# Down phases of an encoder step: block sums made in place, operands prepared earlier, ends re-ordered, and matmuls of a tile ordered by column halves

## The chip, the cores and the metric

The kernel runs on 1 core of one Trainium2 chip. The metric is device time in microseconds (us). TensorE (PE in the rows; PEld are its weight loads), VectorE (DVE), ScalarE (ACT), GpSimd (POOL) and SyncE (SP, which only issues transfers here) each run a program of their own in order and meet at semaphores.

## The reference

Two layers of an encoder over 1024 prompt rows and 32 sample rows (1056 columns here), width 1024. Each layer is a mixer and then a feed-forward part, in fp32:

```
def sq_relu_ffn(h, w1, w2):
    return jnp.square(jax.nn.relu(h @ w1)) @ w2
xp = xp + mp
xp = xp + sq_relu_ffn(rms_norm(xp, norm_ffn_g[i]), w_ffn1[i], w_ffn2[i])   # w1 1024x4096, w2 4096x1024
```

The change lies in the second product (the "down phase") of both layers, and in what follows it: in layer 0 the norm and input projection of the next mixer, in layer 1 the transposes and the output.

## The kernel before, in words

Every fp32 product is made of three float32r matmuls: both operands are split into a high part (ACT copies to float32r) and a low part (the difference), and high·high, high·low and low·high are summed.

**Up phase.** 16 units of 256 hidden rows, two jobs (128 rows) each. SP loads a unit's weights into one half of `stage`, POOL splits them (`split`: four high pieces of 512 columns, then four low ones) into one half of `w_sp`, PE runs 72 matmuls of 352 columns a job (L273), DVE takes the relu and scales it (L433), ACT squares (`squares`, L358). Hidden rows and columns are cut into halves, and DVE forms sums of the blocks (`combine`, L441 to L446) so that the down product takes 7 block products instead of 8 (Strassen–Winograd). SP stores a unit's 8 blocks in memory (`hid_spill`, 2112 KB).

**Down phase.** 8 chunks of K; a chunk has 7 block products q, each of 4 tiles m, so 28 tiles. A tile (`down_tile`, L317) is 12 matmuls of 264 columns into a pair of PSUM banks; the four pairs are used in turn. For each chunk:

- SP loads two stage halves of weights (`down_weights`, L1996) once POOL has made the low part for q = 6 of the chunk before, and then the hidden blocks (`hidden`, L2000), each once PE is done with that q.
- POOL (`split_down`) makes the sums of weight blocks that a q needs (two 512-column sums, L2136 to L2142) and the low parts of the weights (L2149). ACT makes the high parts (`w_high`, L371) and those of the hidden blocks (`b_high`, L376); DVE makes the low parts of the hidden blocks (`b_low`, L460).
- DVE adds each finished tile to its target (`down`, L468 and L470), x in `xT` or one of three sums in `aux`. PE may be at most four tiles ahead of it (`pt_free`).

The engines' programs are written out by hand, so the order is that of the code. ACT's `prepare` handles `w_high(c, q)`, then `b_high(c, q - 1)`. DVE has one or two `b_low` behind the four `down` of a q: in chunk 0 behind q = 4 it has `b_low(7)` and `b_low(8)`, which belong to q = 0 and 1 of chunk 1, and behind q = 5 `b_low(9)` and `b_low(10)`.

Sums for q = 2, 3 and 6 go to two buffers `Sx`, which lie over `rstd`, the scale that DVE still reads for the last up unit; so POOL waits there for both of its jobs. The operands for q = 2 and 3 lie over the `w_sp` half of the last or the last but one up unit; those for q = 6 lie over the buffer from which the last up unit is stored.

**The last chunk** runs its tiles by m: all 7 q for m = 0, then m = 1 and so on (`LAST`). When DVE has the seven, it and POOL (`combine_last`, L2164 to L2170) add up the block sums of that m. DVE's seventh `down` waits for all four of POOL's additions. In layer 0 POOL runs `split(U_OIN)`, which prepares the weights of the next projection, ahead of all `combine_last`. SP loads these weights behind the last `down_weights`. ACT and DVE put the next norm's squares and the split of x between (`act_n2`, `dve_n2`).

Of the kernel before, what the change touches and what calls it, by code (L numbers as in the profile page):

```python
# [74 lines left out]
BLK = [0, 2, 4, 5, 6, 7, 3]  # L75
S_AT = {2: 0, 3: 1, 4: 2, 6: 3}
# [3 lines left out]
SC_S = sum(P * (b + 1) for b in range(2, 8))  # L80

# [6 lines left out]
def build_encoder(nc, dram):  # L88
    ctx = ExitStack()
    with ctx:  # L90
# [123 lines left out]
        cb, cb_u, cb_x = sem("cb"), sem("cb_u"), sem("cb_x")  # L214
# [66 lines left out]
        def gemm_in_unit(pe, u, j, widths=(P, P), du=0, dj2=0, blk=None, rhs=lambda k, b: h[:, k, b, :]):  # L281

            pe.wait_ge(w_split, u + 1 + du)
            for t, m in enumerate(widths):
                gemm_tile(pe, j + t, u % 2, KT, t * P, 256, m, rhs, dj2,
                          blk if t == 0 else None)

        def pe_up(pe, u0, j0, blkh, times):
            pe.wait_ge(w_split, u0 + 1)
            gemm_tile(pe, j0, u0 % 2, KT, 0, 256, P, ffn_h, blk=blkh)  # L290
# [7 lines left out]
            gemm_tile(pe, j0 + 1, u0 % 2, KT, P, 256, P, ffn_h)  # L298
# [11 lines left out]
        def down_tile(pe, L, t, q, m, dt=0):  # L310
# [35 lines left out]
        LAST = [0, 1, 2, 3, 4, 5, 6]  # L346

        def act_ffn(act, L, j0):
# [5 lines left out]
            def squares(i, d=0):  # L354
                for t in range(2):
                    evacuated(act, j0 + 2 * i + t, d)
                    x = ob[i % 2][:, 2 * t:2 * t + 2, :]
                    act.activation(x, x, ACT.Square).then_inc(s_done, 1)  # L358

            def w_high(c, q, d=0):  # L360

                K = NCHK * L + c
                slot = (L + 0) % 2
                for i in range(2):
                    st = stage[:, (slot + i) % 2, :]
# [4 lines left out]
                    x = {0: st[:, 0:512], 1: st[:, 1024:1536], 4: st[:, 512:1024], 5: st[:, 1536:2048]}.get(q, Sx[i][:, :])  # L370
                    act.activation(w2[q][i][:, 0, :], x, ACT.Copy).then_inc(wh_done, 1)  # L371
# [16 lines left out]
            squares(0)  # L388
            with act.Fori(0, 7) as i:
                for t in (1, 2):  # L390
                    squares(t + 0, i * 2)
            for q in (0, 1):
                w_high(0, q)
            for q in (0, 1):
# [269 lines left out]
        def dve_n2(dve, ch):  # L664
# [1666 lines left out]
```

## Time and profile before

| what | value |
|---|---|
| median of 3 runs | 2571.79 us (2571.58 to 2573.43) |
| the profiled execution: its own time | 2571.93 us |
| its span in the trace | 2570.2 us |
| mean granted clock of TensorE | 0.983 of full speed |
| PE busy | 2456.9 us (96%), 17227 matmuls |
| POOL busy | 1413.0 us (55%) |
| DVE busy | 1456.5 us (57%) |
| ACT busy | 777.5 us (30%) |

Layer 0's down phase begins at about 928 us of the span and layer 1's at about 2199 us. PE's busy time of 96% hides stretches in which it stands still; they are in the rows below. A clock of 1.00 in a row is 2.4 GHz, 0.50 is 1.2 GHz.

### The profile page before, as it was taken

How to read it: one execution, taken by the hardware profiler on the slowest of the kernel's cores; microseconds unless marked ns; L12 is line 12 of the kernel's file. 1: busy time of each engine (PE TensorE's matmuls, PEld its weight loads, DVE VectorE, ACT ScalarE, POOL GpSimd, SP SyncE). 2: the span in 40 equal slices, each digit the busy share in tenths (PEclk: the TensorE clock that was granted, in tenths of full speed). 3: DMA queues.
4: the chain of work that ended last, by engine and by line, in shares of the span. 5: the costliest groups of instructions: out<-in, count | busy, mean ns of one | idle time of the engine just before them, and what ended most of it. 6: DMA issues, size and time to landing. Idle time of an engine off the chain costs nothing.

```text
span 2570.2 us, 42362 instructions
## 1 busy us (share of the span) xinstructions
PE 2456.9 (96%) x17227; PEld 2322.9 (90%) x17227; DVE 1456.5 (57%) x1988; ACT 777.5 (30%) x1164; POOL 1413.0 (55%) x1035
## 2 busy tenths in 40 slices
PE   8999999999999997999889999989999999799998
PEld 7998866999999997999878998669999999799998
DVE  4333389444333465776668878763433343667676
ACT  4200277211010123333237832652110101243431
POOL 4433256245444558787751333953554454688785
PEclk9999999999999998999999998999999999999999
DMA  6111110213344444445140111002134433444441
GB/s 221 34 50 35 69 66 2 84 50 134 123 143 150 149 154 142 158 125 158 55 141 23 50 34 55 18 17 101 46 138 150 150 127 140 193 125 143 158 126 77
DMA packets 128201, 264.10 MB, mean 103 GB/s; under 512 B 15517, under 2 KB 81141, under 8 KB 123478
## 3 DMA queue, kind: packets, MB, share of 16 engines
q1 hardware_dynamic: 125446, 245.17, 28.2%
q10 hardware_dynamic: 2640, 17.31, 1.7%
q8 instruction: 83, 1.36, 0.2%
q14 instruction: 32, 0.26, 0.0%
HBM read 173.72 MB, written 87.93 MB: 102 GB/s over the span
## 4 chain that ended last, share of the span: by engine, by line
PE 62%; POOL 17%; issue 11%; DVE 7%; ACT 2%; DMA 0%; POOLq 0%; SPq 0%; DVEq 0%; ACTq 0%
PE PS L273 49%; POOL w L2149 9%; POOL Sx L2142 2%; POOL Sx L2138 1%; PE PS L1097 1%; PE PS L1158 1%; POOL Sx L2136 1%; PE PS L1508 1%; PE PS L317 1%; PE PS L1135 1%; POOL stage L2140 1%; PE PS L1537 1%; PE PS L1477 1%; POOL Lb L1872 1%; PE PS L780 1%
## 5 line engine op out<-in xcount | busy, mean ns | idle before, releaser
L273 PE MATMUL PS<-h,w_sp 128*128 128x352 f32 (+1 forms) x5184 | 857.1, 325 | 16.2 <-DVE h L726 6.6
L273 PEld LDWEIGHTS PS<-h,w_sp 128*128 128x128 f32 (+1 forms) x5184 | 839.3, 188 | 23.3 <-issue 18.0
L2104 POOL TENSOR_TENSOR w_sp<-stage,ones 128x512 fp32r<-128x512 f32 x244 | 268.2, 1131 | 835.8 <-PE PS L273 788.8
L317 PE MATMUL PS<-Bq,w 128*128 128x264 f32 x5376 | 667.3, 287 | 51.1 <-DVE xT L470 42.5
L317 PEld LDWEIGHTS PS<-Bq,w 128*128 128x128 f32 x5376 | 664.2, 191 | 54.1 <-issue 26.6
L273 PE MATMUL PS<-hz,w_sp 128*128 128x352 f32 x3456 | 567.0, 323 | 0.0
L273 PEld LDWEIGHTS PS<-hz,w_sp 128*128 128x128 f32 x3456 | 557.7, 188 | 0.0
L2108 POOL TENSOR_TENSOR w_sp<-stage,w_sp 128x512 fp32r<-128x512 f32 x244 | 368.6, 1542 | 0.0
L433 DVE SCALAR_TENSOR_TENSOR ob<-PS,rstd 128x1056 f32<-128x1056 f32 x64 | 80.5, 1258 | 400.1 <-PE PS L273 400.1
L358 ACT ACTIVATE ob<-ob 128x1056 f32<-128x1056 f32 x64 | 69.6, 1088 | 643.7 <-DVE ob L433 643.7
L2149 POOL TENSOR_TENSOR w<-stage,w 128x512 fp32r<-128x512 f32 x128 | 191.6, 1520 | 131.4 <-ACT w L371 131.2
L470 DVE TENSOR_TENSOR xT<-PS,xT 128x528 f32<-128x528 f32 x256 | 177.9, 704 | 109.8 <-PE PS L317 85.4
L460 DVE TENSOR_TENSOR Bq<-Bq 128x1056 fp32r<-128x1056 f32 x112 | 177.1, 1585 | 37.0 <-ACT Bq L376 37.0
L470 DVE TENSOR_TENSOR aux<-PS,aux 128x528 f32<-128x528 f32 x168 | 117.9, 704 | 65.7 <-PE PS L317 65.6
L2149 POOL TENSOR_TENSOR w<-Sx,w 128x512 fp32r<-128x512 f32 x96 | 139.3, 1471 | 0.0
L376 ACT ACTIVATE Bq<-Bq 128x1056 fp32r<-128x1056 f32 x112 | 119.3, 1074 | 40.1 <-PE PS L317 36.7
L371 ACT ACTIVATE w<-Sx 128x512 fp32r<-128x512 f32 x96 | 60.8, 633 | 215.2 <-POOL Sx L2136 72.3
L1234 POOL TENSOR_TENSOR sg<-sg,kept 128x1024 f32<-128x1024 f32 (+3 forms) x45 | 82.2, 1829 | 63.3 <-DVE kept L1204 63.0
L973 DVE TENSOR_TENSOR Z<-PS,rstd 128x1056 f32<-128x1056 f32 x20 | 25.1, 1257 | 159.7 <-PE PS L273 155.3
L371 ACT ACTIVATE w<-stage 128x512 fp32r<-128x512 f32 x128 | 75.1, 626 | 129.4 <-DMA stage<-in_w_ffn 69.7
L1571 ACT ACTIVATE reach<-score,bs__92 128x1024 bf16<-128x1024 f32 (+2 forms) x96 | 99.0, 1033 | 12.8 <-DVE bs__92 L1717 12.2
L1704 DVE TENSOR_SCALAR_CACHE_REDUCE reach<-score,bs__92 128x640 bf16<-128x640 f32 (+3 forms) x128 | 88.6, 745 | 1.6 <-DVE bs__92 L1694 0.2
(307 smaller groups left out, 2310.6 us busy)
## 6 DMA issues: line engine op xcount, KB each, us to landing
hid_spill<-ob SPq DMA_DIRECT2D x32, 2112.0 KB, 7.6
stage<-in_w_ffn SPq DMA_DIRECT2D x64, 1024.0 KB, 7.5
Bq<-hid_spill SPq DMA_DIRECT2D x112, 528.0 KB, 3.8
stage<-in_w_in_even SPq DMA_DIRECT2D x10, 1024.0 KB, 4.8
stage<-in_w_in_odd SPq DMA_DIRECT2D x9, 1024.0 KB, 5.0
x_spill<-xT ACTq DMA_DIRECT2D x2, 4224.0 KB, 12.6
xT<-x_spill ACTq DMA_DIRECT2D x2, 4224.0 KB, 12.5
xtok<-in_x_prompt SPq DMA_DIRECT2D x8, 512.0 KB, 8.9
```

Of the source, the lines that this page charges most:

```text
L273: mm = pe.matmul(out[0:m, c, :], lhs, rhs(k, b)[:, c * CH:(c + 1) * CH], start=(i == 0 and n == 0), stop=(i == nk - 1 and n == 2))
L317: mm = pe.matmul(out[:, c, :], w2[q][i][:, a, m * P:(m + 1) * P], Bq[q][:, b, i, c * QN:(c + 1) * QN], start=(i == 0 and n == 0), stop=(i ...
L371: act.activation(w2[q][i][:, 0, :], x, ACT.Copy).then_inc(wh_done, 1)
L376: act.activation(Bq[q][:, 0, :, :], B_raw[q][:, :, :], ACT.Copy).then_inc(bh_done, 1)
L460: dve.tensor_tensor(Bq[q][:, 1, :, :], B_raw[q][:, :, :], Bq[q][:, 0, :, :].bitcast(F32), ALU.subtract).then_inc(bl_done, 1)
L470: ins = dve.tensor_tensor(x, src, x, ALU.add)
L1234: pool.tensor_tensor(w, w, x[:, :, c0 + 1:c0 + 1 + n], ALU.mult).then_inc(a_w, 1)
L1571: act.activation(reach[:, r], score[:, r], ACT.Sign, scale=-1.0, bias=bs_[:, n % 2, bi:bi + 1], accum_out=bs_[:, 2, bi:bi + 1]).then_inc(a ...
L1704: ch.mark(dve.tensor_scalar(reach[0:m, r], score[0:m, r], bs_[0:m, now, bi:bi + 1], 0.0, ALU.is_lt, ALU.add, accum_out=bs_[0:m, CNT, bi:bi ...
L2104: pool.tensor_tensor(w_sp[:, s, 0, q:q + 512], stage[:, s, q:q + 512], ones[:, 0:1].to_broadcast([P, 512]), ALU.mult).then_inc(w_hi_done, 1)
L2108: lo = pool.tensor_tensor(w_sp[:, s, 1, q:q + 512], stage[:, s, q:q + 512], w_sp[:, s, 0, q:q + 512].bitcast(F32), ALU.subtract)
L2149: pool.tensor_tensor(w2[q][i][:, 1, :], x, w2[q][i][:, 0, :].bitcast(F32), ALU.subtract).then_inc(wl_done, 1)
```

## The change

In words:

- **Block order.** The products are renumbered (`BLK`, `S_AT`, new `A_AT`): q = 0, 1, 2 now take a weight block as it lies in `stage`, q = 3 to 6 take sums, and these are made in place in `stage`; `Sx` is gone.
- **Stage half and `w_sp` half** of a unit come from `wslot`, which swaps the halves from U_OIN on. The operands for q = 2 and 3 now lie over the `w_sp` half of the last unit but one in both layers, so that ACT waits for two jobs less (`job_done, j0 + 30`).
- **Last up unit.** ACT squares its two halves between `w_high` steps, and POOL, not DVE, makes its four sums (`last_combine`), between its steps for q = 5 and q = 6.
- **Column order.** In `down_tile` the loop over the two column halves (banks) moves from innermost to outermost.
- **Last chunk.** `LAST` puts q = 2 next to last. DVE's last `down` of an m waits for three of POOL's additions and no longer for the fourth. In layer 0 POOL runs `combine_last(0)`, the high half of `split(U_OIN)`, `combine_last(1)`, the low half, and the other two. SP loads U_OIN one step later. The norm's additions and x splits on DVE are placed differently, and PE waits for one `pt_free` less.

The diff, cut:

```diff
-BLK = [0, 2, 4, 5, 6, 7, 3]
-S_AT = {2: 0, 3: 1, 4: 2, 6: 3}
+BLK = [0, 2, 7, 4, 5, 6, 3]
+S_AT = {3: 0, 4: 1, 5: 2, 6: 3}
+A_AT = [0, 2, 3, 3, 3, 1, 3]
+def wslot(u):
+    return (u + (u >= U_OIN)) % 2
...
-            for i in range(2):
-                for n, (a, b) in enumerate(((0, 0), (0, 1), (1, 0))):
-                    for c in range(2):
+            for c in range(2):
+                for i in range(2):
+                    for n, (a, b) in enumerate(((0, 0), (0, 1), (1, 0))):
                         mm = pe.matmul(out[:, c, :], w2[q][i][:, a, m * P:(m + 1) * P],
...
-        LAST = [0, 1, 2, 3, 4, 5, 6]
+        LAST = [0, 1, 3, 4, 5, 2, 6]
...
-            squares(15)
-            act.wait_ge(job_done, j0 + 32)
+            act.wait_ge(job_done, j0 + 30)
             w_high(0, 2)
             w_high(0, 3)
-            for q in range(2, 6):
-                b_high(0, q)
-            b_high(0, 6)
+            square(15, 0)
             act.wait_ge(hid_st[0], 16 * (8 * L + 8))
             w_high(0, 4)
             w_high(0, 5)
+            square(15, 1)
+            for q in range(2, 7):
+                b_high(0, q)
             act.wait_ge(hid_st[1], 16 * (8 * L + 8))
             w_high(0, 6)
...
-                    if q == 0 and m == 1:
-                        combine(15)
-                for n in ((2,), (3, 4), (5, 6), (), (7, 8), (9, 10), (11,))[q]:
+                for n in ((2,), (3,), (4,), (5, 6), (7, 8), (9, 10), (11,))[q]:
                     b_low(n)
...
-                dve.wait_ge(cb, 16 * L + 4 * m + 4)
+                dve.wait_ge(cb, 16 * L + 4 * m + 3)
                 down(t0 + 6, 6, m)
...
-                                evacuated(pool, (J_F0, J_F1)[L] + 30)
-                                evacuated(pool, (J_F0, J_F1)[L] + 31)
...
+            def last_combine(L):
+
+                x, n = ob[1], 4 * (16 * L + 15)
+                pool.wait_ge(s_done, 2 * (16 * L + 15) + 2)
+                pool.tensor_tensor(x[:, 4, :], x[:, 1, :], x[:, 0, :], ALU.subtract).then_inc(t_done, 1)
+                pool.tensor_tensor(x[:, 6, :], x[:, 3, :], x[:, 1, :], ALU.subtract).then_inc(t_done, 1)
...
+            def down_all(L):
+                split_down(0, L, qs=range(6))
+                last_combine(L)
+                split_down(0, L, qs=(6,))
...
-            down_all(0, U_F0)
-            split(U_OIN)
-            combine_last(0)
+            down_all(0)
+            pool.wait_ge(job_done, J_F0 + 32)
+            combine_last(0, 0)
+            split_high(U_OIN)
+            combine_last(0, 1)
+            split_low(U_OIN)
+            combine_last(0, 2)
+            combine_last(0, 3)
```

How the programs stand, first POOL at the beginning of layer 0's down phase, before (`w_2_0` is the operand for q = 2, K half 0; `Sx` the sum buffers):

```order
L2149 TENSOR_TENSOR w_1_1_66<-stage,w_1_1_66 128x512
L2136 TENSOR_TENSOR Sx_77<-stage 128x512
L2136 TENSOR_TENSOR Sx_78<-stage 128x512
L2149 TENSOR_TENSOR w_2_0_67<-Sx_77,w_2_0_67 128x512
L2149 TENSOR_TENSOR w_2_1_68<-Sx_78,w_2_1_68 128x512
L2138 TENSOR_TENSOR Sx_77<-Sx_77,stage 128x512
L2138 TENSOR_TENSOR Sx_78<-Sx_78,stage 128x512
```

and the same stretch, up to q = 6, in the changed kernel:

```order
L2151 TENSOR_TENSOR w_2_0_67<-stage,w_2_0_67 128x512
L2151 TENSOR_TENSOR w_2_1_68<-stage,w_2_1_68 128x512
L2141 TENSOR_TENSOR stage<-stage 128x512 x2
...
L2151 TENSOR_TENSOR w_5_0_73<-stage,w_5_0_73 128x512
L2151 TENSOR_TENSOR w_5_1_74<-stage,w_5_1_74 128x512
L2158 TENSOR_TENSOR ob_52<-ob_52 128x528
L2159 TENSOR_TENSOR ob_52<-ob_52 128x528
L2161 TENSOR_TENSOR ob_52<-ob_52 128x528
L2163 TENSOR_TENSOR ob_52<-ob_52 128x528
L2147 TENSOR_TENSOR stage<-stage 128x512 x2
L2151 TENSOR_TENSOR w_6_0_75<-stage,w_6_0_75 128x512
```

The low parts for q = 2 now follow at once, and the four sums of the last up unit (`ob_52`) stand ahead of q = 6.

POOL at the end of layer 0's down phase, before (`w_sp` is the split of the next projection's weights):

```order
L2104 TENSOR_TENSOR w_sp<-stage,ones 128x512 x4
L2108 TENSOR_TENSOR w_sp<-stage,w_sp 128x512 x4
L2164 TENSOR_TENSOR xT<-xT,aux 128x528
L2165 TENSOR_TENSOR xT<-xT,aux 128x528
L2168 TENSOR_TENSOR xT<-xT,aux 128x528
L2170 TENSOR_TENSOR xT<-xT,aux 128x528
```

and in the changed kernel:

```order
L2179 TENSOR_TENSOR xT<-xT,aux 128x528
L2180 TENSOR_TENSOR xT<-xT,aux 128x528
L2183 TENSOR_TENSOR xT<-xT,aux 128x528
L2185 TENSOR_TENSOR xT<-xT,aux 128x528
L2109 TENSOR_TENSOR w_sp<-stage,ones 128x512 x4
L2179 TENSOR_TENSOR xT<-xT,aux 128x528
```

The additions for m = 0 have moved ahead of the split, whose halves now stand behind m = 0 and m = 1.

## Rows read from the trace of the kernel before

**Rows 1.** PE by stretch: length, busy us (matmuls), granted clock, DMA share, GB/s

```profile
927.80:990.50 62.70, 43.62 (x338) 0.91 0.47 172
1000.00:1040.00 40.00, 40.00 (x332) 1.00 0.47 145
1237.80:1310.30 72.50, 56.09 (x409) 0.91 0.16 56
2199.30:2260.70 61.40, 43.46 (x338) 0.90 0.47 176
2507.80:2553.90 46.10, 41.55 (x337) 0.98 0.04 12
```

**Rows 2.** Timeline, start of layer 0's down phase: start, us, what, count [idle before]

```profile
907.80 6.46 POOL L2149 TENSOR_TENSOR w<-stage,w 128x512 fp32r<-128x512 f32 x4 [15.18 <-ACT w L371]
...
929.37 2.56 POOL L2136 TENSOR_TENSOR Sx<-stage 128x512 f32<-128x512 f32 x2 [15.10 <-issue]
...
937.66 0.36 SPq L1985 DMA_DIRECT2D hid_spill<-ob  x1
...
956.40 2.55 POOL L2149 TENSOR_TENSOR w<-Sx,w 128x512 fp32r<-128x512 f32 x2
...
957.73 1.62 SPq L1996 DMA_DIRECT2D stage<-in_w_ffn  x2
...
966.39 1.67 ACT L371 ACTIVATE w<-stage 128x512 fp32r<-128x512 f32 x3 [3.33 <-DMA stage<-in_w_ffn]
...
969.07 1.65 DVE L460 TENSOR_TENSOR Bq<-Bq 128x1056 fp32r<-128x1056 f32 x1 [6.18 <-ACT Bq L376]
...
978.61 7.68 PE L317 MATMUL PS<-Bq,w 128*128 128x264 f32 x48 [10.66 <-DVE xT L470]
...
990.47 19.71 PE L317 MATMUL PS<-Bq,w 128*128 128x264 f32 x140 [4.18 <-DVE xT L470]
```

**Rows 3.** DMA issues of 935 to 970 us: count, KB, us to landing

```profile
hid_spill<-ob SPq DMA_DIRECT2D x1, 2112.0 KB, 6.4
```

**Rows 4.** The page's groups: count, busy us, mean ns of one, idle before

```profile
L470 DVE TENSOR_TENSOR xT<-PS,xT 128x528 f32<-128x528 f32 x256 | 177.9, 704 | 109.8 <-PE PS L317 85.4
L460 DVE TENSOR_TENSOR Bq<-Bq 128x1056 fp32r<-128x1056 f32 x112 | 177.1, 1585 | 37.0 <-ACT Bq L376 37.0
...
L376 ACT ACTIVATE Bq<-Bq 128x1056 fp32r<-128x1056 f32 x112 | 119.3, 1074 | 40.1 <-PE PS L317 36.7
```

**Rows 5.** POOL's low parts by source line: ns min/median/max

```profile
L2149 POOL TENSOR_TENSOR w<-stage,w x128: 1265/1299/2315, 907.8 to 2505.0; 128x512 fp32r<-128x512 f32 x128
```

**Rows 6.** Timeline, end of layer 0's down phase

```profile
1245.69 5.55 POOL L2104 TENSOR_TENSOR w_sp<-stage,ones 128x512 fp32r<-128x512 f32 x4 [2.38 <-DMA stage<-in_w_in_odd]
...
1256.11 1.29 POOL L2164 TENSOR_TENSOR xT<-xT,aux 128x528 f32<-128x528 f32 x1
...
1261.38 0.71 DVE L470 TENSOR_TENSOR xT<-PS,xT 128x528 f32<-128x528 f32 x1 [11.30 <-POOL xT L2170]
...
1262.14 23.64 PE L317 MATMUL PS<-Bq,w 128*128 128x264 f32 x180 [9.83 <-DVE xT L470]
...
1298.01 11.76 PE L273 MATMUL PS<-h,w_sp 128*68 128x352 f32 x72 [2.75 <-issue]
...
1310.26 1.98 PE L705 MATMUL PS<-rstd,ones 128*128 128x512 f32 x4 [0.49 <-DVE rstd L675]
```

**Rows 7.** Timeline, end of layer 1's down phase

```profile
2552.51 0.71 DVE L470 TENSOR_TENSOR xT<-PS,xT 128x528 f32<-128x528 f32 x1 [1.70 <-POOL xT L2170]
...
2553.88 10.63 PE L2293 MATMUL PS<-ident,xT 128*128 128x128 f32 x72 [3.63 <-DVE xT L470]
```

**Rows 8.** Timeline of PE and PEld: eight matmuls of one bank (L1372), 18 rotating (L273)

```profile
924.89 3.04 PE L273 MATMUL PS<-h,w_sp 128*128 128x352 f32 x18
...
1343.87 1.26 PEld L1372 LDWEIGHTS PS<-h,w_sp 128*128 128x128 f32 x8 [0.76 <-issue]
...
1343.87 1.55 PE L1372 MATMUL PS<-h,w_sp 128*128 128x352 f32 x8
```

More of the change, by code:

```diff
@@ L352, in act_ffn, with square @@
                                scale=1.0 / D).then_inc(rt_done, 1)
[L354 to L358, printed above, removed]
+            def square(i, t, d=0):
+                evacuated(act, j0 + 2 * i + t, d)
+                x = ob[i % 2][:, 2 * t:2 * t + 2, :]
+                act.activation(x, x, ACT.Square).then_inc(s_done, 1)
             def w_high(c, q, d=0):
                 K = NCHK * L + c
-                slot = (L + 0) % 2
                 for i in range(2):
-                    st = stage[:, (slot + i) % 2, :]
                     if q in S_AT:
@@ L386, in prepare @@
                         b_high(c, q - 1, d)
-            squares(0)
+            for i in range(1):
+                square(0, 0)
+                square(0, 1)
             with act.Fori(0, 7) as i:
[L390 to L394, printed above, removed]
-                b_high(0, q)
-            squares(15)
-            act.wait_ge(job_done, j0 + 32)
+                for n in (1, 2):
+                    square(n, 0, i * 2)
+                    square(n, 1, i * 2)
+            w_high(0, 0)
+            w_high(0, 1)
+            b_high(0, 0)
+            b_high(0, 1)
+            act.wait_ge(job_done, j0 + 30)
             w_high(0, 2)
             w_high(0, 3)
-            for q in range(2, 6):
-                b_high(0, q)
-            b_high(0, 6)
+            square(15, 0)
             act.wait_ge(hid_st[0], 16 * (8 * L + 8))
@@ L496, in dve_ffn, with last @@
                     b_low(7 + q + 5, i)
-            def last(m, before=()):
+            def last(m, one=None, two=None):
                 t0 = 196 + 7 * m
                 own = PT_L * L + t0
+                step = 4 * L + m + 1
                 a1, a5, a6 = (aux[:, m, x, :] for x in range(3))
@@ L505, in last @@
                 down(t0 + 1, 1, m)
-                down(t0 + 2, 2, m)
-                down(t0 + 3, 3, m)
+                down(t0 + 2, 3, m)
+                if one is not None:
+                    one()
+                down(t0 + 3, 4, m)
                 if m == 0:
@@ L523, in dve_ffn @@
             for m in range(4):
-                last(m)
-                if between is not None:
-                    between(m)
+                if between is None:
+                    last(m)
+                else:
+                    last(m, *between[m])
+            if between is not None:
+                between[4]()
         def x_tile_ready(eng, n, m):
@@ L1423, in pe_odd @@
             pe.wait_ge(w_split, U_OIN + 2)
[L1424 removed]
+            gemm_tile(pe, J_OI + 2, wslot(U_OIN + 1), KT, 0, 256, P, hh, between=kip_turns)
             evacuated(pe, J_OI + 1)
@@ L2192, in _ @@
             split_ffn(1, U_F1, 5)
-            down_all(1, U_F1)
-            combine_last(1)
+            down_all(1)
+            for m in range(4):
+                combine_last(1, m)
         @block.scalar
```

166 lines of the change are left out of this document (79 added, 87 removed).

## The prediction

> **What bounds the kernel now.** I read the windows of PE first, since they show where PE loses time. In the middle of a down phase it loses none: 332 matmuls in 40.00 us at full clock are 0.1205 us each, and busy is the whole window [rows 1]. A tile of 12 costs 1.45 us and a chunk of 28 tiles 40.5 us. Against that stand four stretches at the ends of the phases [rows 1]:
>
> - start of layer 0's phase up to the moment when chunk 1 begins: 62.7 us for one chunk, 22.2 too long;
> - the same in layer 1: 61.4 us, 20.9 too long;
> - layer 0's last chunk up to the norm's sum matmul: 72.5 us. It holds 40.5 us of tiles and the first job of the next projection, 11.8 us [rows 6], so 20.2 are lost;
> - layer 1's last chunk up to the transposes: 46.1 us, 5.6 lost.
>
> Together 68.9 us, which is also the most that the change can give there, apart from the clock and the output tail.
>
> The timeline then says who is late. In chunk 0 PE stands for 10.66 and 4.18 us for a DVE addition [rows 2]. That is PSUM room and no late operand: DVE is in order, and its additions for q = 5 and 6 stand behind `b_low` of chunk 1, where it waits (6.18 us at 969.07) for ACT's high parts. ACT has these behind `w_high` of chunk 1, for which it waited for the stage, whose transfers SP could issue only at 957.73, when POOL made the low parts for q = 6 of chunk 0 (956.40) [rows 2]. And POOL was late since it had waited 15.10 us, until 929.37, for the last up unit to be read before it could use Sx [rows 2]. So the chain is POOL, SP, DMA, ACT, DVE, PE.
>
> At layer 0's end POOL runs `split(U_OIN)` first: it waits for the transfer until 1245.69 and reaches the additions for m = 0 only at 1256.11. DVE waits 11.30 us for the fourth of them and PE 9.83 us for DVE [rows 6]. In layer 1 there is no split, and each m costs DVE a wait of some 1.7 us for POOL's fourth addition [rows 7].
>
> **The change, start of a phase.** Durations: POOL 1.3 us for a piece of 512 columns [rows 5], 1.28 for a sum (2.56 for two) [rows 2], 1.3 for 528 columns [rows 6]; ACT 0.56 (1.67 for three) [rows 2] and 1.07 [rows 4]; DVE 0.70 and 1.6 [rows 4].
>
> POOL has q = 0 and 1 done at 914.3 (907.80 + 6.46) and goes on: q = 2 to 917.2; sums and lows of q = 3 to 922.4, of q = 4 to 927.6, sums for q = 5 to 930.2, its lows to 932.8. ACT keeps up (its wait is now for jobs that end at about 904), and squares the second half of unit 15 at 931 to 932. POOL's four sums then end at 932.8 + 4 × 1.3 = 938.1, so SP's store goes at 938.3, hardly later than now (937.66) [rows 2]. It lands 6.4 us later [rows 3], at 944.8; only then may ACT write the operand for q = 6, which lies over that buffer. POOL's lows for q = 6 are done at 946.9 and 948.2 instead of 957.7 and 959, so both stage transfers go nearly 10 us earlier.
>
> Now the same chain for chunk 1. The stage halves landed about 4.7 and 8.6 us after the first issue (ACT started on the second half at 966.39, 3.33 us after it had finished the first) [rows 2]: 951.5 and 955. ACT: four high parts to 956.8, `b_high(0)` 957.9, q = 2 needs no sum, `b_high(1)` 960.2. DVE has finished q = 4 of chunk 0 at 957.8 and then makes `b_low(7)` to 959.7 and `b_low(8)` to 961.9, before q = 5 ends on PE at 962.6: the 10.66 us stall is gone. Then `b_low(9)` needs `b_high` of q = 2, behind `w_high` of q = 3, whose sum POOL has at 964.7: done at 968.2. `b_low(10)` needs POOL's sum for q = 4 (970.0), ACT to 971.8, DVE to 973.5. Only then come the additions for q = 6. PE ends chunk 0 at 968.4, is four tiles ahead and stands until 974.2. So **chunk 1 begins at 974.2 to 976 instead of 990.5; I take 974.9: −15.6 us.** In layer 1 it is 47.1 us after the phase's start instead of 61.4: **−14.3 us.** One stall of 6 us costs clock like one of the two of today (0.91 in this window [rows 1]); I take no difference.
>
> The unknown here is POOL's pace. Its pieces take from 1.265 to 2.315 us [rows 5]. At the low end of a fast pace the stall would shrink to some 3 us (gain 18 each); if the 20-odd pieces from 914 to 970 ran a third slower, chunk 1 would begin 6 to 7 us later (gain 8 to 9 each).
> The Trainium skill (GPSIMD Engine Reference, Specifications) says that GpSimd shares its SBUF interfaces with VectorE and contends with VectorE instructions that have two SBUF inputs. By that rule, POOL's pieces beside DVE's low parts and sums are the slow ones, and those beside DVE's additions out of PSUM are not; by the slow price alone each start would gain 8 rather than 15. The spread in [rows 5] agrees with it, and its median is near the minimum.
>
> Moved with it: DVE is freed of the four sums, which stood between its first additions; POOL has the same number of pieces per chunk as before (8 sums, 14 lows, about 28 us of 40.5), so the middle stays at PE's pace.
>
> **End of layer 0's phase.** Count from PE's start on the last chunk (1237.8). DVE frees the first three tiles at +6.3, POOL adds to +8.9 and, after DVE's sum of aux, its third to about +11; DVE's last addition of m = 0 is done at about +14 instead of +24.3 (1262.1) [rows 6]. PE, four tiles ahead, loses 0.4 us instead of 9.83. POOL's high half of the split (5.55 us [rows 6]) goes +14 to +19.5, m = 1 to +23.4, the low half to +30.3, m = 2 to +34.2: PE would want these by +25.0 and +35.2, so they are hidden, narrowly. If POOL is 1 us later per half, PE waits 1 to 2 us. The transfer of U_OIN goes 1.3 us later, but POOL wants it at +14 and it lands at about +10. PE finishes its tiles at +41; DVE, which has two `square` and low(2) before its last additions, lets PE into the projection at +45.3, and seven lows and three sums of 1.25 to 1.3 us follow: n2's sum matmul at +58.8 instead of +72.5 [rows 6]: **−13.7 us** (11 to 16).
>
> **End of layer 1's phase.** Without the fourth addition in the wait and with no other work, PE ends at +40.6, DVE at +41.3, the transposes begin at +42.0 instead of +46.1 [rows 7]. Behind it comes the output, whose pace doesn't change, but the transposes start warmer: **−5.0 us** (3 to 6.5).
>
> **Column order.** The 5376 matmuls are the same, each with its weight load. What changes is that six in a row add into one bank instead of alternating. The nearest row is L1372, eight in a row into one bank with the weights changing as here: (1.55 − 0.32)/7 = 0.175 us each by PE's rows, (1.26 − 0.19)/7 = 0.153 by the weight loads'; rotating over three banks it is (3.04 − 0.32)/17 = 0.160 [rows 8] (0.32 and 0.19 being one instruction's own length). The first contains a start-up after an idle gap, the second a load issued ahead; I take the middle, no difference: **0 us.** The ends are −4.5% and +9% of 5376 × 0.1205 = 648 us: −29 and +58 us.
> The Trainium skill (Perfetto Trace Analysis, Matmuls) says that an accumulation group targets one bank by construction and that independent groups should rotate through banks. Here the pair rotates in both orders, so by that page this edit costs nothing, where the upper row would cost 58 us.
>
> **Sum.** 15.6 + 14.3 + 13.7 + 5.0 = 48.6 us off 2571.93 (the profiled execution, 0.1 above the median of 2571.79, so nothing to correct): **2523.3 us, I say 2524.**
>
> **Rivals.**
> - *Starts gain half.* POOL's longer path (its four sums beside DVE's `b_low(2)` at 2.3 us instead of 1.3, and the pieces behind) delays the stage again: 8 to 9 us each start, total 48.6 − 12 = 36, at 2536. For it: the maxima in [rows 5]; against: the median. 0.20.
> - *The split becomes the bound at layer 0's end.* Two hidden pieces have less than 1.5 us to spare. If both miss and the projection waits, that end gains 6 instead of 13.7: 2531. 0.10.
> - *The second start-up stall vanishes too* (the lows faster than my chain, as DVE no longer disturbs POOL): 3 us more each and less clock lost, 2516. 0.08.
> - *Same bank costs.* Consecutive accumulation slows each matmul. It eats the whole gain at 48.6/5376 = 9 ns a matmul (7.5%); by the 0.175 row it would be +58 − 48.6 = +9 us, 2581: slower than before. For it: that row; against: it begins with a gap, and the weight loads of the same eight show none. 0.04.
> - *Same bank helps*, as the weight loads' row taken literally: 2523 − 29 = 2494. 0.03.
> - Forecast: 0.55.
>
> **How the numbers follow.** The range leaves out the two bank cases and the far parts of the others: 2511 to 2541. What a measurement can tell from no change is about 0.2%, 5 us. Faster by more than that: all but the same-bank loss and an unforeseen wait, 0.93; same 0.03; slower 0.04.
>
> **What the profile after would show.** No POOL wait of 15 us before its sums; SP's stage issue at about 20.5 us after the phase's first matmul instead of 30; one PE stall of 5 to 7 us instead of 10.66 and 4.18, ending 46 to 48 us after the start; the middle still 332 matmuls in 40 us; in layer 0's last chunk no PE wait over 2 us before one of about 4 at the projection; the norm's matmul 59 us into that chunk; transposes 42 us into layer 1's. Wrong if: the middle's pace is not 332 (column order); the stage issue comes at 25 or later (POOL); or a new wait of PE for `wl_done` (PEld for POOL) shows.

## The result and the profile after

The changed kernel takes 2544.23 us (median of 4 runs, 2544.21 to 2545.37), the kernel before 2572.61 us beside it (2571.58 to 2576.79). The ratio is 0.9888 with a 95% interval of 0.9871 to 0.9905: faster by 28.4 us or 1.1%. The forecast was 2524 (2511 to 2541), so the sign was right and the time 3 us outside the range. The profiled execution spans 2542.5 us against 2570.2.

The windows of PE in the kernel after, in the columns of [rows 1]: start of layer 0's phase to chunk 1, last chunk to the norm's sum matmul, start of layer 1's phase to chunk 1.

```profile
927.10:980.10 53.00, 42.93 (x338) 0.94 0.56 203
1227.60:1292.80 65.20, 55.81 (x409) 0.95 0.18 63
2182.80:2233.70 50.90, 41.55 (x338) 0.96 0.59 212
```

With exact first matmuls the span splits as follows (us; the last column is how far the kernel after stayed behind the forecast):

| stretch | before | after | change | forecast | short by |
|---|---|---|---|---|---|
| up to layer 0's phase | 927.8 | 927.1 | -0.65 | 0 | -0.65 |
| layer 0, start to chunk 1 | 62.7 | 53.0 | -9.7 | -15.6 | 5.9 |
| chunks 1 to 6 | 247.1 | 247.4 | +0.3 | 0 | 0.3 |
| last chunk to norm matmul | 72.7 | 65.3 | -7.4 | -13.7 | 6.3 |
| to layer 1's phase | 889.0 | 890.0 | +1.0 | 0 | 1.0 |
| layer 1, start to chunk 1 | 61.4 | 50.9 | -10.5 | -14.3 | 3.8 |
| chunks 1 to 6 | 246.9 | 248.6 | +1.7 | 0 | 1.7 |
| last chunk and output | 62.6 | 60.2 | -2.4 | -5.0 | 2.6 |
| sum | 2570.2 | 2542.5 | -27.7 | -48.6 | 20.9 |

The start of layer 0's phase in the timeline after, POOL first (these answer to [rows 2]):

```profile
907.15 11.00 POOL L2151 TENSOR_TENSOR w<-stage,w 128x512 fp32r<-128x512 f32 x6 [15.18 <-ACT w L372]
918.11 2.54 POOL L2141 TENSOR_TENSOR stage<-stage 128x512 f32<-128x512 f32 x2
...
937.14 2.23 POOL L2163 TENSOR_TENSOR ob<-ob 128x528 f32<-128x528 f32 x1
939.32 3.64 POOL L2147 TENSOR_TENSOR stage<-stage 128x512 f32<-128x512 f32 x2
...
959.14 8.28 POOL L2151 TENSOR_TENSOR w<-stage,w 128x512 fp32r<-128x512 f32 x5 [2.17 <-ACT w L372]
967.39 2.52 POOL L2141 TENSOR_TENSOR stage<-stage 128x512 f32<-128x512 f32 x2
...
972.37 3.52 POOL L2143 TENSOR_TENSOR stage<-stage 128x512 f32<-128x512 f32 x2
```

and of SP, ACT, DVE and PE there:

```profile
939.39 0.36 SPq L1986 DMA_DIRECT2D hid_spill<-ob  x1
949.86 1.62 SPq L1997 DMA_DIRECT2D stage<-in_w_ffn  x2
...
947.84 1.15 ACT L372 ACTIVATE w<-stage 128x512 fp32r<-128x512 f32 x2 [9.69 <-DMA hid_spill<-ob]
...
962.19 4.11 DVE L465 TENSOR_TENSOR Bq<-Bq 128x1056 fp32r<-128x1056 f32 x2 [4.73 <-ACT Bq L378]
977.56 1.89 DVE L465 TENSOR_TENSOR Bq<-Bq 128x1056 fp32r<-128x1056 f32 x1 [4.04 <-ACT Bq L378]
...
967.06 7.45 PE L322 MATMUL PS<-Bq,w 128*128 128x264 f32 x48 [4.49 <-DVE xT L475]
980.12 5.07 PE L322 MATMUL PS<-Bq,w 128*128 128x264 f32 x26 [5.60 <-DVE xT L475]
```

POOL's 15 us wait ahead of its sums is gone, and the stage goes out 22.7 us after the phase's start instead of 29.9. But several pieces are longer than the forecast took them: six lows 11.00 us instead of 6 x 1.3 = 7.8, a pair of sums 3.52 or 3.64 instead of 2.56, five lows 8.28 instead of 6.5, DVE's low parts 1.9 to 2.1 each instead of 1.6. The store went at 939.39 and ACT could go on only at 947.84.

They are not longer than in the kernel before, whose timeline has the same lengths in the same stretch:

```profile
935.32 3.44 POOL L2138 TENSOR_TENSOR Sx<-Sx,stage 128x512 f32<-128x512 f32 x2
941.23 3.56 POOL L2140 TENSOR_TENSOR stage<-stage 128x512 f32<-128x512 f32 x2
...
951.88 4.57 POOL L2142 TENSOR_TENSOR Sx<-stage,Sx 128x512 f32<-128x512 f32 x2
```

There POOL's 16 pieces from 929.37 to 956.45 took 27.2 us, 1.7 us each and not 1.3.

The end of layer 0's phase:

```profile
1242.78 4.04 POOL L2109 TENSOR_TENSOR w_sp<-stage,ones 128x512 fp32r<-128x512 f32 x4
...
1253.33 6.55 POOL L2117 TENSOR_TENSOR w_sp<-stage,w_sp 128x512 fp32r<-128x512 f32 x4
...
1265.15 7.57 PE L322 MATMUL PS<-Bq,w 128*128 128x264 f32 x60 [2.19 <-DVE xT L475]
1278.81 14.19 PE L278 MATMUL PS<-h,w_sp 128*68 128x352 f32 x72 [6.08 <-DVE xT L475]
1292.84 1.88 PE L707 MATMUL PS<-rstd,ones 128*128 128x512 f32 x4
```

The wait of 9.83 us [rows 6] is gone. What is left is 2.19 us inside the chunk and 6.08 us before the projection, whose 72 matmuls take 14.19 us instead of 11.76: up to 1284.2 the granted clock is down at 0.51 of full speed, the 1.2 GHz level. The window of PE there, which begins within that wait:

```profile
1277.30:1284.20 6.90, 5.39 (x19) 0.51 0.00 0
```

DVE's last sum of squares, which the norm's matmul at 1292.84 also needs, was done 1.2 us ahead of it, at 1291.62:

```profile
1289.02 2.60 DVE L687 TENSOR_TENSOR rstd<-rstd,sqb 128x1056 f32<-128x1056 f32 x2
```

At the end of layer 1 one wait stands, and its releaser is new. DVE's own last additions ended within 0.02 us of it:

```profile
2525.86 1.32 DVE L475 TENSOR_TENSOR xT<-PS,xT 128x528 f32<-128x528 f32 x2
2525.90 1.30 POOL L2185 TENSOR_TENSOR xT<-xT,aux 128x528 f32<-128x528 f32 x1 [1.39 <-DVE xT L523]
2527.93 8.05 PE L2314 MATMUL PS<-ident,xT 128*128 128x128 f32 x72 [2.96 <-POOL xT L2185]
```

### The profile page after: what moved, and what is told of

Read it like the earlier page. It is cut to its first block, busy times and chain, and to the rows that moved or that the text cites. A ratio compares the mean times of both kernels' runs of the same rounds, so it can differ in the third digit from the quotient of the medians.

```text
span 2542.5 us, 42346 instructions
## 1 busy us (share of the span) xinstructions
PE 2453.5 (96%) x17227; PEld 2319.7 (91%) x17227; DVE 1459.4 (57%) x1980; ACT 777.3 (31%) x1164; POOL 1414.4 (56%) x1043
## 4 chain that ended last, share of the span: by engine, by line
PE 63%; POOL 18%; issue 10%; DVE 6%; ACT 1%; DMA 1%; POOLq 0%; SPq 0%; ACTq 0%; DVEq 0%
PE PS L278 51%; POOL w L2151 9%; PE PS L1099 1%; POOL stage L2143 1%; POOL stage L2141 1%; PE PS L1160 1%; POOL stage L2145 1%; PE PS L1510 1%; PE PS L1137 1%; POOL stage L2147 1%; PE PS L1539 1%; PE PS L1479 1%; PE PS L322 1%; POOL Lb L1874 1%; DMA hid_spill<-ob 1%
## 5 line engine op out<-in xcount | busy, mean ns | idle before, releaser
L2151 POOL TENSOR_TENSOR w<-stage,w 128x512 fp32r<-128x512 f32 x224 | 349.6, 1583 | 142.6 <-ACT w L372 142.5
L372 ACT ACTIVATE w<-stage 128x512 fp32r<-128x512 f32 x224 | 135.8, 628 | 374.8 <-PE PS L322 83.9
L465 DVE TENSOR_TENSOR Bq<-Bq 128x1056 fp32r<-128x1056 f32 x112 | 183.3, 1639 | 26.9 <-ACT Bq L378 26.8
L1874 POOL TENSOR_SCALAR Lb<-Lb,st 128x128 f32<-128x128 f32 (+8 forms) x72 | 54.9, 774 | 46.2 <-DVE st L1813 46.2
L575 DVE TENSOR_TENSOR xT<-PS,xT 128x1056 f32<-128x1056 f32 x16 | 20.1, 1255 | 72.1 <-PE PS L278 46.8
```

The source lines that it names most:

```text
L372: act.activation(w2[q][i][:, 0, :], stage[:, i, 512 * A_AT[q]:512 * A_AT[q] + 512], ACT.Copy).then_inc(wh_done, 1)
L465: dve.tensor_tensor(Bq[q][:, 1, :, :], B_raw[q][:, :, :], Bq[q][:, 0, :, :].bitcast(F32), ALU.subtract).then_inc(bl_done, 1)
L2151: pool.tensor_tensor(w2[q][i][:, 1, :], stage[:, i, 512 * A_AT[q]:512 * A_AT[q] + 512], w2[q][i][:, 0, :].bitcast(F32), ALU.subtract).then ...
```

## The experiments

Theory: the chain and its order are as forecast, and the shortfall is the price of POOL and DVE working beside each other, with something for the column order. Rivals: the landing of the store and of hidden blocks; the places of the order at which something else gets late.

### Column order, both ways

In one kernel the changed code gets the old loops, in the other the kernel before gets the new ones:

```diff
-            for c in range(2):
-                for i in range(2):
-                    for n, (a, b) in enumerate(((0, 0), (0, 1), (1, 0))):
+            for i in range(2):
+                for n, (a, b) in enumerate(((0, 0), (0, 1), (1, 0))):
+                    for c in range(2):
```

> The changed kernel with the column halves innermost again, as before. Theory: the new order costs each of the 5376 matmuls of the down phases about 0.55 ns (121.9 ns start to start in the middle of a phase against 121.3), 3 us in all; this kernel then takes 2541 us and a 40 us window in the middle of a phase holds 332 matmuls instead of 330 or 331. Rival: the order is free and the pitch differs for another reason (POOL and DVE now work differently beside PE): 2544 us and 330 or 331 matmuls.

> The kernel before with only the loop over column halves moved outermost. Theory: 3 us slower, 2575 us, and 330 to 331 matmuls in 40 us. Rival: no difference, 2572 us and 332. If it is 9 us or more slower, the order also disturbs the starts of the phases.

Measured: the old order in the changed kernel 2543.62 us (2539.73 to 2544.0; 0.9878 of before, 0.9863 to 0.9893), which doesn't differ from 0.9888 within the intervals. The new order alone 2577.47 against 2573.05 beside it (11 runs; 1.0014, 1.0005 to 1.0023): slower by 3.6 us. The windows of PE from 1030 to 1230 us, in which PE never waits, show it more sharply. They are, in this order, before, new order alone, after, and after with the old order:

```profile
1030.00:1230.00 200.00, 200.00 (x1651) 1.00 0.47 147
```
```profile
1030.00:1230.00 200.00, 200.00 (x1643) 1.00 0.46 145
```
```profile
1030.00:1230.00 200.00, 200.00 (x1644) 1.00 0.45 145
```
```profile
1030.00:1230.00 200.00, 200.00 (x1650) 1.00 0.44 144
```

Old order 121.1 and 121.2 ns a matmul, new order 121.7 both times: 0.5 ns more, 3 us over 5376. A chunk in the middle of a phase agrees: 40.8 us in both kernels with the old order, 41.0 in both with the new one, in both layers. Six matmuls in a row into one bank cost a little, 0.4% and not the 9% of the prediction's upper bound.

### The end of layer 0's phase undone

```diff
-            pool.wait_ge(job_done, J_F0 + 32)
+            split(U_OIN)
             combine_last(0, 0)
-            split_high(U_OIN)
             combine_last(0, 1)
-            split_low(U_OIN)
             combine_last(0, 2)
             combine_last(0, 3)
```

> The changed kernel with the whole split of the next projection's weights ahead of all of POOL's additions in layer 0's last chunk again. Theory (the split in front is what PE waited 9.83 us for): the norm's sum matmul comes 7 to 9 us later in the last chunk than in the changed kernel, 2552 us. Rival (DVE's and POOL's shared work sets that end, whatever stands in front): within 3 us, 2545 us.

Measured: 2552.53 us (0.9916, 0.9901 to 0.9931), 7.2 us more by the ratios (0.0028 of 2573). PE's wait is back at its old place, and the norm's matmul comes 73.2 us into the last chunk instead of 65.3:

```profile
1253.08 21.16 PE L322 MATMUL PS<-Bq,w 128*128 128x264 f32 x156 [10.52 <-DVE xT L475]
```

So the split's place is what that end gained.

### POOL's wait put back

```diff
                     if q in S_AT:
+                        if len(qs) == 6 and q == 3:
+                            evacuated(pool, (J_F0, J_F1)[L] + 30)
+                            evacuated(pool, (J_F0, J_F1)[L] + 31)
```

> The changed kernel with one thing put back: POOL waits for DVE to have read the last up unit's two jobs (after 929) before the first of its sums in chunk 0, as it did in the kernel before; the new block table, the sums in the stage and all of the ends' rearrangement stay. Theory (it is POOL's place in the chain POOL, SP, DMA, ACT, DVE, PE that the starts gained): each start loses most of its gain again, the stage issue comes at +27 to +30 after the phase's first matmul instead of +22.7 and +21.0, chunk 1 begins at +58 to +62 instead of +53.0 and +50.9, and the time is 2556 to 2564. Rival (the starts gained because the order of blocks and of ACT's and DVE's work changed, and POOL's early wait was hidden): no change, 2544.

Measured: 2565.88 us (0.9966, 0.9953 to 0.998), 20 us more than after by the ratios. Chunk 1 begins 63.8 and 62.5 us after the phases' starts. Its timeline:

```profile
928.73 2.55 POOL L2144 TENSOR_TENSOR stage<-stage 128x512 f32<-128x512 f32 x2 [10.57 <-DVE ob L438]
...
960.69 1.62 SPq L1997 DMA_DIRECT2D stage<-in_w_ffn  x2
```

The wait of 10.57 us moves the stage by 960.69 - 949.86 = 10.8 us and chunk 1 by 10.8 (layer 1: 11.6). The theory's numbers were too small: 2556 to 2564 us, chunk 1 at +58 to +62, and the stage issue at +27 to +30, where it came at +33.6. That is later even than in the kernel before (+29.9), and so is chunk 1 (62.7 and 61.4 there): the one wait gives back all that the starts had gained. POOL's first sum, the stage issue and chunk 1 moved by 10.6, 10.8 and 10.8 us in layer 0, so the link from POOL to SP to PE holds to some 0.2 us.

### Small additions on POOL at the ends

```diff
-                pool.tensor_tensor(x11, x11, a1, ALU.add).then_inc(cb, 1)
+                pool.tensor_tensor(x11[:, 0:8], x11[:, 0:8], a1[:, 0:8], ALU.add).then_inc(cb, 1)
```

and the same in the other three additions of `combine_last`.

> Leaves out part of the work: POOL's additions of the last chunk cover 8 columns of 528, in both layers. Theory (at the ends GpSimd and VectorE slow each other): DVE's sums of two SBUF operands, 1.1 to 1.8 us each there, fall to 0.71, and PE has no stall in layer 0's last chunk but the one ahead of the projection; the last chunk up to the norm's matmul takes 59 to 61 us instead of 65.7 and up to the transposes 42.5 instead of 45.1; 2535 us. Rival (their times come from something else): DVE's sums keep their length and the ends gain under 3 us together.

Measured: 2533.87 us (0.9849, 0.9832 to 0.9865), 10 us less than after by the ratios. The norm's matmul comes 56.6 us into the last chunk (after 65.3, forecast 58.8), the transposes 42.6 into layer 1's (after 45.6, forecast 42.0), and PE waits nowhere within the chunks. What DVE's own additions cost tells why. First the same line in the kernel after, then in this one (ns, least/median/most):

```profile
L517 DVE TENSOR_TENSOR aux<-aux x8: 1078/1752/1818, 1236.9 to 2521.4; 128x528 f32<-128x528 f32 x8
```
```profile
L517 DVE TENSOR_TENSOR aux<-aux x8: 694/708/709, 1235.6 to 2510.0; 128x528 f32<-128x528 f32 x8
```

DVE's instruction is the same; only POOL's neighbours shrank. What happens is plain in this kernel's timeline, where POOL's additions of 8 columns take 0.20 us, except beside a `square` sum of DVE (L687):

```profile
1255.47 0.20 POOL L2183 TENSOR_TENSOR xT<-xT,aux 128x8 f32<-128x8 f32 x1 [1.22 <-DVE aux L517]
1257.57 1.15 POOL L2185 TENSOR_TENSOR xT<-xT,aux 128x8 f32<-128x8 f32 x1 [1.90 <-DVE xT L523]
...
1257.41 1.25 DVE L687 TENSOR_TENSOR rstd<-rstd,sqb 128x1056 f32<-128x1056 f32 x1
```

DVE's sum ran from 1257.41 to 1258.66; POOL's addition began at 1257.57 and ended at 1258.72, with the same 8 columns as the one of 0.20 us. It stood until DVE was done. So the two engines don't share a rate here: an instruction of one with both inputs in SBUF waits for the whole instruction of the other, and the wait is inside its duration. Rows of the kernel after can be read so (DVE, then POOL):

```profile
1234.93 2.04 DVE L465 TENSOR_TENSOR Bq<-Bq 128x1056 fp32r<-128x1056 f32 x1
1236.89 1.82 DVE L517 TENSOR_TENSOR aux<-aux 128x528 f32<-128x528 f32 x1
...
1234.54 1.32 POOL L2179 TENSOR_TENSOR xT<-xT,aux 128x528 f32<-128x528 f32 x1 [0.83 <-DVE aux L475]
1235.81 2.33 POOL L2180 TENSOR_TENSOR xT<-xT,aux 128x528 f32<-128x528 f32 x1
```

POOL has the memory until 1235.86, so DVE's low part ends at 1236.97 (2.04 long); POOL's next waits for that and ends at 1238.14 (2.33 long); DVE's sum ends only then, at 1238.71 (1.82 long). From end to end that is 1.11, 1.17 and 0.57 us for work of 1.24, 1.3 and 0.71 alone: one after another, with only some 0.13 us of each overlapped. The Trainium skill (SBUF — State Buffer, SBUF: two separate sides) states this as a lock that is exclusive for the whole instruction, taken by whoever starts first, between GpSimd's operations that read SBUF and VectorE's with two SBUF inputs. These rows agree with it.

A wait can span more than one instruction. At the start of layer 0's phase, in the kernel after, a low part of DVE that takes 1.24 us alone took 4.39, while POOL ran three sums without a gap, the last of them up to 937.06:

```profile
933.79 4.39 DVE L465 TENSOR_TENSOR Bq<-Bq 128x1056 fp32r<-128x1056 f32 x1
...
935.75 1.31 POOL L2161 TENSOR_TENSOR ob<-ob 128x528 f32<-128x528 f32 x1
```

By the rule as the Trainium skill states it, DVE, which had begun before POOL's second sum, would have had its turn at 934.47, behind the first; the rows have it behind the third.

### Small low parts on DVE at the starts

```diff
                 for n in ((2,), (3,), (4,), (5, 6), (7, 8), (9, 10), (11,))[q]:
-                    b_low(n)
+                    b_low(n, w=8)
```

> The changed kernel, in which DVE's low parts for the ten blocks that it makes during chunk 0 are taken on 16 of 528 columns only (the rest of them is left out, so the products of these blocks are wrong); everything else, and every wait, stays. So DVE's instructions with two SBUF inputs are nearly gone from the stretch in which the start fell short. Theory (GpSimd's pieces are slow beside them: the sums of two took 3.5 us instead of 2.6, the lows 1.8 instead of 1.3): POOL's sums come back to 1.3 us each, the stage issue comes at +21 or before, chunk 1 begins at +46 to +49, and the time is 2535 to 2539. Rival A (POOL's pace does not hang on DVE's low parts): POOL's pieces stay as slow as now, the start gains only the two or so us of DVE's own work, chunk 1 begins at +50 to +52, and the time is 2541 to 2543. Rival B (the start is bound by the store's and the hidden blocks' landing): +53 and +51, 2544.

(The slice is 128x16 out of 128x1056, 8 columns in each half.) Measured: chunk 1 begins 48.4 and 46.1 us after the starts, where the forecast of the change had 47.1 and the kernel after 53.0 and 50.9. POOL's rows are back at their own length:

```profile
938.49 1.33 POOL L2163 TENSOR_TENSOR ob<-ob 128x528 f32<-128x528 f32 x1
939.77 2.54 POOL L2147 TENSOR_TENSOR stage<-stage 128x512 f32<-128x512 f32 x2
...
959.97 6.25 POOL L2151 TENSOR_TENSOR w<-stage,w 128x512 fp32r<-128x512 f32 x5 [2.89 <-ACT w L372]
966.17 2.52 POOL L2141 TENSOR_TENSOR stage<-stage 128x512 f32<-128x512 f32 x2
...
971.14 2.56 POOL L2143 TENSOR_TENSOR stage<-stage 128x512 f32<-128x512 f32 x2
```

2.23 became 1.33, 3.64 and 3.52 became 2.54 and 2.56, 8.28 became 6.25. The starts are 4.6 and 4.8 us shorter, but the whole time doesn't confirm the 2535 to 2539: its four runs scatter from 2538.03 to 2553.98 (median 2542.44; 0.9892, 0.987 to 0.9914, no different from after), and the profiled one, with a span 6.2 us under that of after, was the fastest of them. So the verdict rests on the rows. Some of the gain is DVE's own shorter work, which this kernel doesn't part from POOL's. In layer 0 the stage still goes out at +21.9, since the store's landing is what it was (8.4 us).

### The store in two halves, and the four sums on DVE

```diff
-                store(15)
+                sp_.wait_ge(s_done, 2 * (16 * L + 15) + 2)
+                sp_.dma_start(hid_rows[:, 15:16, 0:4 * HN], ob_row[1][:, :, 0:4 * HN]).then_inc(hid_sq, 16)
+                sp_.wait_ge(t_done, 4 * (16 * L + 15) + 4)
+                sp_.dma_start(hid_rows[:, 15:16, 4 * HN:8 * HN], ob_row[1][:, :, 4 * HN:8 * HN]).then_inc(hid_st[1], 16)
+                sp_.wait_ge(hid_sq, 16 * (L + 1))
```

> The changed kernel with the last up unit stored in two halves: the four squared blocks as soon as ACT has them, the four sums (which the operand for q = 6 overwrites) when POOL has them. Theory (the landing of this store, 8.4 us in layer 0 and 6.4 in layer 1, stands on the chain to chunk 1's operands): the high parts for q = 6 start 2.5 to 4 us earlier, chunk 1 begins 2 to 4 us earlier in each layer, 2538 us. Rival (the store is hidden, or the first half pushes the hidden blocks' loads back by as much): 2543 to 2545 us.

> The changed kernel with the four sums of the last up unit on DVE again, between its first additions, as before. Theory (POOL's part is no help in itself: they end at 12.3 us after the phase's start on POOL, at 9.9 on DVE before): the store goes 2 us earlier, and chunk 1 begins 0 to 2 us earlier, but PE has its three stalls of 1 to 1.8 us in chunk 0 again, which the later stall absorbs: 2541 to 2545 us. Rival (taking them off DVE is what shortened the start): chunk 1 begins 3 us later or more in each layer, 2550 us.

Measured: 2540.63 us for the halves (0.9873, 0.9857 to 0.9890), 2542.45 with the sums on DVE (0.9883, 0.9867 to 0.9900). Chunk 1 begins at 51.2 and 48.9 with the halves, at 50.7 and 50.9 with the sums on DVE. That is some 2 us less at both starts or at one, which the intervals of the whole time can't tell from nothing and which is not far beyond the scatter of the starts themselves: 52.5 to 53.7 us in layer 0 and 50.9 to 52.1 in layer 1 in four kernels whose starts are alike but for the column order. With the halves, ACT goes on 2.7 us earlier in layer 0, so the landing is on the chain. What its 2 extra us cost there was not run by itself. With the sums on DVE the store landed in 6.8 us instead of 8.4 in layer 0 and in an unchanged 6.4 in layer 1, and the starts moved by 2.3 and 0.0 us, which speaks for some 2 us.

### Holding DVE's low parts back

DVE made the low parts for chunk 1 between its additions for chunk 0, and PE stood for it. In one kernel they are made three blocks later in chunk 0 and caught up in chunk 1; in the other they stay late until chunk 6 (the diff, cut, is the second's; its first two lines are in both):

```diff
-                for n in ((2,), (3,), (4,), (5, 6), (7, 8), (9, 10), (11,))[q]:
+                for n in ((2,), (3,), (4,), (5, 6), (), (7,), (8, 9))[q]:
...
-                    b_low(7 + q + 5, i)
+                    for n in ((10,), (11,), (12,), (13,), (), (14,), (15, 16))[q]:
+                        b_low(n, i)
```

> The changed kernel with DVE's low parts for chunk 1 taken out from between the additions of chunk 0: q = 0 behind q = 5's additions, q = 1 and 2 behind q = 6's, and those behind spread over chunk 1. Theory A (the stalls of PE at a phase's start are room in PSUM: DVE waits for ACT's high parts with finished tiles behind it, while the operands themselves come in time): both stalls go in both layers, chunk 1 begins 41 to 43 us after the phase's first matmul instead of 53.0 and 50.9, and the time falls by 17 to 21 us to about 2525. Theory B (the operands of chunk 1 are themselves late, since POOL takes 6.0 us for a q that has a sum): PE waits as long, only for another semaphore, 2541 to 2545 us.

> The changed kernel with DVE's low parts behind the additions by a lead of three products instead of five in chunks 0 to 5 (chunk 0: none behind q = 4, q = 0 of the next behind q = 5, q = 1 and 2 behind q = 6; chunks 1 to 5 the same with q = 3 to 6 of their own behind q = 0 to 3), and caught up in chunk 6. e5 moved the stalls from chunk 0 into chunk 1, where DVE again waited for a high part of the next chunk with finished tiles behind it. Theory A (queue order on DVE alone, operands come in time once it no longer runs five ahead): no stall over 1 us in chunks 0 to 6; every chunk 41.0 us instead of 53.0 and 42.7 in layer 0 and 50.9 and 43.8 in layer 1; 2544 - 26 = 2518 us. Theory B (the stage is single and POOL's pace makes chunk 2 late): stalls come back in chunk 1 or 2 for another reason, 2535 to 2544 us.

Measured: caught up in chunk 1, 2543.45 us (0.9881, 0.9866 to 0.9896): chunk 0 takes 41.1 us and chunk 1 53.1, so the wait only moves. Caught up in chunk 6, 2537.26 (2534.07 to 2545.58; 0.9866, 0.9843 to 0.9889), where theory A had 2518 and theory B 2535 to 2544 with stalls in chunk 1 or 2. The time is B's, but the stall is elsewhere. Chunks 0 and 1 take 41.1 and 41.6, which shows that the stalls at the start were PSUM room, held by DVE's order, and no late operand. But in the last chunk, whose first seven tiles need all seven blocks of operands, PE waits again:

```profile
1229.45 20.77 PE L322 MATMUL PS<-Bq,w 128*128 128x264 f32 x155 [4.89 <-DVE aux L475]
```

I read this wait as the supply's: stage, ACT and POOL turn over a chunk's weights in 39.7 us at first (stage issues at 949.36 and 989.05) and in 39.6 on the average of six, against PE's 41.0, so a late start of that chain is made up at 1.3 to 1.4 us a chunk. By this estimate, a lead that PE takes at the start must be given back at the end, less what six chunks make up; no run varied the supply by itself.

### Three parts together

> The changed kernel with three parts that were run alone: the old order of columns (alone 2543.6 against 2544.2, chunks of 40.8 instead of 41.0), the store of unit 15 in two halves (alone 2540.6), and DVE's low parts held back by three blocks in chunks 1 to 5 and caught up in chunk 6 (alone 2537.3). If they add: 2537.3 - 3.6 - 3 = 2531 (2528 to 2534). Rival (at the phases' ends the chain of stage and POOL is the bound after the low parts are held back, so an earlier start and a faster chunk only lengthen the wait of 5 us at tile 200): 2535 to 2538.

> The combined kernel with SP's work of chunk 1 in another order: the first two hidden blocks go before the store of unit 15, and the stage's two transfers right behind the store, ahead of the other hidden blocks. Theory (the wait of ACT's first high part of hidden state for the block's transfer, until 961 in layer 0, and the stage issue behind the blocks hold the chain back): 2 to 3 us less than the combined kernel, if that is not bound by its end. Rival (the blocks arrive before POOL's and ACT's parts are done, or the end gives it back): the same as the combined kernel within 1 us.

The first is the changed kernel with the old column order, the store in halves and the low parts held back until chunk 6. The second also has SP's order changed:

```diff
+                for q in range(2):
+                    sp_.wait_ge(pt_done, PT_L * L + 4 * q + 4)
+                    hidden(1, q)
                 sp_.wait_ge(s_done, 2 * (16 * L + 15) + 2)
```

with `down_weights(2)` and `(3)` right behind the store. Measured: 2529.12 us (2526.65 to 2533.55; 0.9823, 0.9810 to 0.9837) for the first. That is within the 2528 to 2534 of the parts added, and below the rival's 2535 to 2538. It beats both kernels: 45 us under the one before (2574.14 beside it) and some 17 under the changed one by the ratios. In layer 0 PE has no gap over 0.6 us until chunk 6, and then the supply's:

```profile
927.58 87.61 PE L323 MATMUL PS<-Bq,w 128*128 128x264 f32 x719
...
1228.51 30.24 PE L323 MATMUL PS<-Bq,w 128*128 128x264 f32 x228 [4.91 <-DVE aux L476]
```

The second took 2540.93 (0.9873, 0.9858 to 0.9888), 13 us worse by the ratios. The theory was wrong about it: SP is in order, and waiting for PE's tiles of q = 1 it issues the first half of the store only at 940.08, beside the second, and the stage at 952.66 instead of 948.59:

```profile
928.00 12.03 SPq L2008 DMA_DIRECT2D Bq<-hid_spill  x7
940.08 0.47 SPq L2039 DMA_DIRECT2D hid_spill<-ob  x1
...
952.66 2.60 SPq L2004 DMA_DIRECT2D stage<-in_w_ffn  x2
```

That is 4 us of the chain in layer 0, of which 1.0 us is left at the norm's matmul. Most of the loss is in layer 1, where chunk 6 takes 47.7 us instead of 42.4. There too the stage is late from the start: it goes out 23.8 us after the phase's first matmul instead of 18.7, and for the last chunk 261.7 instead of 254.6. Why the lag costs more in layer 1 than in layer 0 was not run down.

## Why the prediction had the chain right and the time wrong

- **What bounds the kernel, and the chain at the starts.** Right. Putting POOL's wait back moved the stage and chunk 1 by 10.8 us each, and with DVE's low parts held back the stalls in chunk 0 were gone, so they were PSUM room as said.
- **The starts, -15.6 and -14.3.** Measured -9.7 and -10.5. The step that failed is the cost of a piece: "POOL 1.3 us for a piece of 512 columns [rows 5], 1.28 for a sum", and "DVE 0.70 and 1.6", of which 1.6 is a low part. Measured beside each other, pieces of POOL took 1.7 to 1.8 us and low parts of DVE 1.9 to 2.1. The 1.3 is a median over all stretches, and the maximum of 2.315 beside it I read as a tail; it is the price of a neighbour. The timeline before had the answer in the very stretch of the change, 1.7 us a piece. The prediction did price it, as a rival at 0.20 and in its "a third slower", but its sum left it out. With DVE's low parts nearly gone the starts were 48.4 and 46.1 against the 47.1 forecast. "It lands 6.4 us later" was 8.4 in layer 0, worth some 2 there. "The 10.66 us stall is gone" failed too (4.49 was left in layer 0, 1.18 in layer 1); the stall ahead of chunk 1, which I had at some 6, was 5.60 in layer 0 and 8.22 in layer 1.
- **The end of layer 0, -13.7.** Measured -7.4. The split's place is what gained (undone, 7.9 us come back), and "they are hidden, narrowly" was too hopeful: a `square` of DVE took up to 2.37 us beside POOL, an addition out of SBUF 1.1 to 1.8 instead of 0.71, and the projection began 51 us into the chunk instead of 45.3. With small additions on POOL the norm's matmul was at 56.6 against the forecast 58.8. The term was mis-sized by the same neglect. The lower clock in the projection, which follows that last wait, adds at most 1.2 us, since DVE's sums would have held the norm's matmul to 1291.7 anyway.
- **The end of layer 1, -5.0.** Measured -2.4, of which the last chunk gave only 0.7 (46.3 to 45.6, where the forecast had 42.0) and the output 1.7. I had dropped the fourth addition from the path altogether ("without the fourth addition in the wait"), though the transposes read what it writes and wait for it. That slip cost nothing here: DVE's own last additions ended at the same time. What made both late is again POOL and DVE beside each other; with POOL's additions small the transposes began at +42.6. The 1.7 us of the output are not firm: behind the same wait the 72 transposes took 8.05 us here, 9.72 with the small low parts and 11.01 with the low parts late until chunk 6.
- **The column order, 0.** Measured +3 us, by the windows of both pairs of kernels; the whole time shows it in one pair only. It lies near the chosen point and far from both bounds. The step from the rule on rotating banks (the Trainium skill, Perfetto Trace Analysis, Matmuls) to "this edit costs nothing" was an inference of mine: the rule gives no price, and the measurement decides.
- **The rivals.** "Starts gain half" (36 us) came true for the most part, though only one of POOL's four sums was slow (2.23), and of layer 0's 5.9 us 2.3 fell before the stage issue and 3.6 behind it. "The split becomes the bound" came near in size (a gain of 6 for that end, measured 7.4), but not, as far as the runs tell, in its cause: with POOL's additions small the split stood where it stands here, PE waited nowhere within the chunk, and that end was shorter than forecast. A kernel without the split was not run. Together the two give 48.6 - 12 - 7.7 = 29, where 27.7 was measured; that they agree so well is partly luck. I priced them as excluding each other, though both ends hang on how POOL and DVE get on, and the upper end of the range held only one of them.

Of layer 1's 1.7 us in chunks 1 to 6 the column order explains about 1.0, and chunk 1 the rest (43.8 us against 43.1). The 1.0 us between the layers is within the scatter of that stretch, which took 889.2 us with the small additions and 892.0 with the split in front. Still open is why one store lands 2 us later than the same one before.

## What to carry to other kernels

Before a step is moved to another engine or another time, ask who will then run beside it. A median over the whole kernel mixes pieces with and without a neighbour; the price is read from the timeline of the stretch itself, or from the longest durations of the same group. When two rivals have one cause, price them together. When an instruction is taken out of a wait, follow the data it writes to the next reader, who inherits the wait. And a lead or lag between a supplier and PE is bought back only at the difference of their periods, here some 1.3 us a chunk.

## What the runs showed of the hardware

GpSimd and VectorE instructions with both inputs in SBUF ran one after another: a GpSimd addition of 8 columns took 1.15 us beside a VectorE sum of 1.25, and 0.20 alone; a VectorE addition of 128x528 took 1.75 us (median) beside GpSimd and 0.71 alone. A VectorE low part of 128x1056, 1.24 us alone, took 4.39 while three GpSimd sums ran without a gap. VectorE's additions out of PSUM kept their 0.70 us throughout. Six float32r matmuls of 264 columns in a row into one bank took 0.5 ns more each than the same six with two banks in turn (121.7 against 121.1 ns).
